# A fifth prefetched expert part, routing by token tile, and an fp32 gather in a two-block network kernel

## The chip, the cores and the metric

The kernel is one launch on one core of a Trainium2 chip. The metric is the device time of that launch in microseconds (us). Before the change three runs took 2184.20, 2184.34 and 2190.19 us, median 2184.34.

## What is computed

The input is 256 tokens of width 1024, all in float32. Two blocks of depth 2 run one after the other. The first block is what this change is about. In each of its two layers:

```python
x = layer_norm(ALPHA * x + mixer(x) @ w_o, ln1_g, ln1_b)        # mixer: attention and gated linear attention, or GQA
aff = softmax(x @ router_w)                                     # 16 experts
gates, idx = top_k(aff.T, 32)                                   # each expert picks its 32 tokens
hid = silu(x[idx] @ w1) * (x[idx] @ w3)                         # per expert 1024 x 1024, twice
ffn = scatter_add((hid @ w2) * gates, idx)                      # 1024 x 1024
ple = sigmoid(x @ ple_gate_w + ple_gate_b) * (p @ ple_w)
x = layer_norm(ALPHA * x + ffn + ple, ln2_g, ln2_b)
```

The second block has, per layer, a feed-forward part, a mixer and another feed-forward part, and ends in one RMS norm: `out = x * rsqrt(mean(x*x) + EPS) * final_norm`.

## The kernel before, in words

Tokens lie on the 128 partitions in two tiles (TILES = 2), so x is [128, 2, 1024]. TensorE (PE) multiplies; a product in exact float32 is one `matmul` in the code and shows in the profile as two records with two weight loads. Where a long product would cost too much that way, both factors are split into a high part, rounded to fp32r, and a low part (value minus high part), and three fp32r products are added: high by high, high by low, low by high. ACT makes high parts (casts), DVE makes low parts (subtractions).

**Weights.** An expert has 12 MiB: six parts of 2 MiB, each 128 partitions by 4096 words. Parts 0 and 1 are the halves of w1, 2 and 3 of w3, 4 and 5 of w2. All weights come through a ring of six slots of 2 MiB (`WeightStream`, L181 issues the loads). SP issues the loads in program order; before a load into a slot it waits on the counter `weights_used`, which PE (or DVE, for a split part) advances when a slot has been read. So a load is issued as soon as the unit six places earlier has been read, and the DMA queue then works off what has been issued.

Expert 1 is special. While routing is still under way nothing can free a slot, so some of its parts go aside, into memory that is free at that time (`aside_places`, with `ASIDE = 4`): part 0 and part 1 into the arena (a general scratch area), part 2 into `mix_cols` and the arena, part 3 into a spare unit that is filled much earlier. Expert 1's parts 4 and 5 use the ring.

**Routing** (L2154 to L2204, L2548 to L2600). After the first layer norm PE multiplies p by ple_w (`ple_products`, 4 results of 512 columns), turns x into columns (L495, eight 128x128 transposes a tile, both tiles together), ACT and DVE split the columns (L504, L520), and 24 products of 16 weight columns and 256 moving columns give the logits (L2555). DVE copies them (L2674), PE turns them, DVE and ACT make the softmax, DVE finds the top 32 by four rounds of MAX8 and MATCH_REPLACE8, and makes the one-hot matrices (`make_hot`), first for experts 0 and 1.

**Gather.** Each expert's tokens are picked by a product of x with the one-hot matrix. Before, x is split for it into `rows_hi` (ACT, L2176, two casts of 2.1 us or more) and `rows_lo` (DVE, L2184, four subtractions). `gather_first` (L2439) picks the tokens of experts 0 and 1 by 32 fp32r products of 256 moving columns, where the 64 wanted columns are repeated four times (`REPEATS`). `gather` (L2453) picks those of all 16 experts by 32 fp32r products of 512 columns, in pieces between the first two experts.

**Experts.** `up` (L2275) is 64 products of 32 weight columns by 256 moving columns, four of which run beside each other on the array; `down` (L2297) 16 of 512; `scatter` (L2307) adds the result into PSUM. After experts 7 and 11 a half of the gate product `x @ ple_gate_w` stands (L2354), its bias added by DVE (L2398, two additions of 128x512 for each half) before ACT's sigmoid.

**The end.** `final_norm`: ACT squares the four halves of x and sums them (L2814), POOL makes both roots together (L2819, L734, L735), DVE scales the two tiles (L3806), SP stores each tile (L3789).

## Time and profile before

| what | value |
|---|---|
| median of 3 runs | 2184.34 us |
| profiled execution, its own time | 2185.28 us |
| its span, first to last instruction | 2183.3 us |
| mean granted PE clock | 0.962 |
| PE busy | 1911.9 us, 88% |
| DVE busy | 1059.3 us, 49% |
| ACT busy | 712.3 us, 33% |
| bytes moved by DMA | 624.05 MB |
| DMA idle or slow around the routing of layer 0 | about 133 to 161 us |
| DMA idle or slow around the routing of layer 1 | about 680 to 742 us |
| experts of layer 0, of layer 1 | about 154 to 602 us, about 738 to 1180 us |

Read it by stretch. In the experts the DMA engines move some 427 GB/s without a break and PE waits for weights; from about 1200 us on (the second block) PE is busy nearly throughout and DMA is half idle. A mean over the span says nothing about either.

### The profile page before, as it was taken

To read this page: it belongs to the slowest core of one execution; us is meant where nothing else is said; L and a number is where in the kernel's file an instruction comes from. 1 tells how busy PE (TensorE), PEld (TensorE's weight loads), DVE (VectorE), ACT (ScalarE), POOL (GpSimd) and SP (SyncE) were. 2 spreads that over 40 slices of the span, in tenths; PEclk is the share of its full clock that TensorE was granted. 3 is DMA by queue.
4 is the path that set the end of the run, shared out by engine and by line. 5 is a ranking of instruction groups with operands and counts; after the bars stand their busy time and mean duration, and the time that the engine had idled before them with its cause. 6 is when DMAs were issued, how large, how long until landed. Compare 5 with 4: busy or idle time off the path is not lost. (4 is left out here: it accounts for less than half of the span.)

```text
span 2183.3 us, 32580 instructions
## 1 busy us (share of the span) xinstructions
PE 1911.9 (88%) x13124; PEld 1354.3 (62%) x13140; DVE 1059.3 (49%) x1607; ACT 712.3 (33%) x1096; POOL 75.6 (3%) x137
## 2 busy tenths in 40 slices
PE   9999667676788986676768999999999999999998
PEld 6765224232366542242324888988888888888887
DVE  4761002010077500020103877787777877787776
ACT  5532002020046210020102433565444433565442
POOL 0000000000010000000000000000000000000000
PEclk9999989998999998898999999999999999999999
DMA  7399999999982899999999655436564655446550
GB/s 243 139 381 427 428 428 423 429 424 427 421 343 72 353 426 430 427 424 428 424 428 398 226 177 205 139 136 212 178 206 155 212 174 201 146 136 207 180 201 19
DMA packets 187952, 624.05 MB, mean 286 GB/s; under 512 B 17655, under 2 KB 129369, under 8 KB 163033
## 3 DMA queue, kind: packets, MB, share of 16 engines
q1 hardware_dynamic: 187864, 622.84, 73.6%
q8 instruction: 61, 1.00, 0.2%
q14 instruction: 27, 0.21, 0.0%
HBM read 621.76 MB, written 1.05 MB: 285 GB/s over the span
## 5 line engine op out<-in xcount | busy, mean ns | idle before, releaser
L3028 PE MATMUL psum<-x_both,up_hi 128*128 128x512 f32 x1408 | 352.9, 393 | 2.5 <-DVE x_both L525 2.2
L2275 PE MATMUL psum<-weight_ring,arena 128*32 128x256 f32 x3840 | 249.5, 411 | 106.7 <-DMA weight_ring<-in_w 106.1
L3028 PEld LDWEIGHTS psum<-x_both,up_hi 128*128 128x128 f32 x1408 | 257.4, 188 | 57.4 <-issue 3.3
L2275 PEld LDWEIGHTS psum<-weight_ring,arena 128*32 128x32 f32 x3840 | 123.5, 116 | 233.8 <-DMA weight_ring<-in_w 133.5
L2415 DVE TENSOR_TENSOR arena<-arena,psum 128x256 f32<-128x256 f32 x32 | 13.5, 421 | 450.6 <-PE psum L2275 450.6
L2297 PE MATMUL psum<-weight_ring,arena 128*32 128x512 f32 x1024 | 148.0, 709 | 73.6 <-DMA weight_ring<-in_w 63.6
L3080 DVE TENSOR_TENSOR up_lo<-weight_ring,up_hi 128x2048 fp32r<-128x2048 f32 x84 | 192.1, 2287 | 13.0 <-ACT up_hi L3051 12.8
L3031 PEld LDWEIGHTS psum<-x_both,up_lo 128*128 128x128 f32 x1408 | 189.4, 188 | 13.5
L3031 PE MATMUL psum<-x_both,up_lo 128*128 128x256 f32 x1408 | 193.2, 280 | 0.0
L3092 DVE TENSOR_REDUCE arena<-psum 128x256 f32<-128x512 f32 x176 | 121.5, 690 | 125.3 <-PE psum L3031 124.2
L652 PE MATMUL psum<-w_lo,x_both 128*128 128x384 f32 (+3 forms) x768 | 170.2, 359 | 2.4 <-DVE mix_lo L793 1.2
L3051 ACT CAST up_hi<-weight_ring 128x2048 fp32r<-128x2048 f32 x84 | 160.1, 1906 | 13.6 <-PE psum L3031 13.4
L3072 ACT ACTIVATE arena<-arena 128x256 f32<-128x256 f32 x88 | 36.7, 418 | 385.9 <-DVE arena L3098 385.9
L2419 DVE COPY arena<-psum 128x512 f32<-128x512 f32 x30 | 20.7, 692 | 283.7 <-PE psum L2297 283.7
L652 PE MATMUL psum<-w_hi,x_both 128*128 128x512 f32 (+3 forms) x640 | 149.2, 365 | 3.5 <-ACT w_hi L613 2.4
L652 PEld LDWEIGHTS psum<-w_lo,x_both 128*128 128x128 f32 x768 | 135.2, 188 | 16.7 <-issue 3.6
L2307 PE MATMUL psum<-arena 128*128 128x512 f32 x240 | 120.2, 648 | 22.2 <-ACT arena L2372 22.2
L3000 PE MATMUL psum<-down_hi,hid_hi 128*128 128x512 f32 x336 | 132.0, 393 | 0.0
L3000 PE MATMUL psum<-down_hi,hid_lo 128*128 128x512 f32 x336 | 131.5, 391 | 0.0
L3000 PE MATMUL psum<-down_lo,hid_hi 128*128 128x512 f32 x336 | 130.5, 389 | 0.0
L2297 PEld LDWEIGHTS psum<-weight_ring,arena 128*32 128x32 f32 x1024 | 31.1, 120 | 155.2 <-DMA weight_ring<-in_w 77.9
L652 PEld LDWEIGHTS psum<-w_hi,x_both 128*128 128x128 f32 x640 | 113.2, 188 | 20.1 <-ACT w_hi L613 3.4
(390 smaller groups left out, 2393.7 us busy)
## 6 DMA issues: line engine op xcount, KB each, us to landing
weight_ring<-in_w SPq DMA_DIRECT2D x184, 2048.0 KB, 25.7
weight_ring<-in_ffn_wg SPq DMA_DIRECT2D x44, 1024.0 KB, 6.0
weight_ring<-in_ffn_wu SPq DMA_DIRECT2D x44, 1024.0 KB, 8.6
weight_ring<-in_ffn_wd SPq DMA_DIRECT2D x44, 1024.0 KB, 5.0
weight_ring<-in_w_in SPq DMA_DIRECT2D x14, 1536.0 KB, 6.7
weight_ring<-in_w_o SPq DMA_DIRECT2D x4, 2048.0 KB, 16.2
arena<-in_w SPq DMA_DIRECT2D x4, 2048.0 KB, 14.9
weight_ring<-in_ple_gate_w SPq DMA_DIRECT2D x4, 2048.0 KB, 25.0
```

The lines of the kernel that those rows point to most:

```text
L652: last = pe.matmul(ps[:, bank, 0:width], x_part[:, cc, a * P:(a + 1) * P], w_part[:, c, :], start=cc == 0 and w_part is high and x_part is ...
L2275: last = pe.matmul(ps[j * CAP:(j + 1) * CAP, 4 + k // 2, 0:QW], tokens[:, cc, :], w[c][:, j * QW:(j + 1) * QW], start=cc == 0, stop=cc == ...
L2297: last = pe.matmul(ps[r * CAP:(r + 1) * CAP, 6 + h, :], hc[:, k, r * CAP:(r + 1) * CAP], w[:, r, h, :], start=k == 0, stop=k == 1)
L2307: last = pe.matmul(ps[:, 2 * a + h, :], back[:, a * P:(a + 1) * P], partial[:, h * BANK:(h + 1) * BANK], start=False, stop=False, skip_gro ...
L2419: dve.tensor_copy(partial[:, BANK:], ps[:, 7, :]).then_inc(part_1.sem, 1)
L3000: last = pe.matmul(ps[:, 2 * h + a, :], x_part[:, f, a * P:(a + 1) * P], w_part[:, f, h * BANK:(h + 1) * BANK], start=False, stop=False, s ...
L3028: last = pe.matmul(ps[:, 4 + 2 * f + h, :], w_part[:, f, h, c, :], x_both[:, :, c, :], start=c == 0, stop=False, skip_group_check=True)
L3031: last = pe.matmul(ps[:, 4 + 2 * f + h, 0:SEQ], w_part[:, f, h, c, :], x_hi[:, c, :], start=False, stop=c == DC - 1, skip_group_check=True)
L3051: act.copy(up_hi[:, k % 2], up_weights(k)).then_inc(hi_up.sem, 1)
L3072: act.activation(silu_g[:, k % 2, :], silu_g[:, k % 2, :], ACT.Silu).then_inc(silued.sem, 1)
L3080: dve.tensor_tensor(up_lo[:, k % 2], up_weights(k), up_hi[:, k % 2].bitcast(F32), ALU.subtract).then_inc(lo_up.sem if k % 2 == 0 else used, 1)
L3092: dve.tensor_reduce(joint[:, f, :], ps[:, 4 + 2 * f + h, :].rearrange("p (t q) -> p q t", t=2), AX, ALU.add).then_inc(joined.sem, 1)
```

## The change

1. **Aside parts.** `ASIDE` is 5: expert 1's part 4 goes aside too, half into `x_cols` as soon as the products of the mixer's output are done, half into `ln_params` after the layer norm. Part 0 is issued earlier, behind p in `mix_out_norm` (its place in the arena is free there because p moved). Expert 0's part 5, the last of the ring before the first expert, is issued last; the slot that it waits for is that of ple_w, whose fourth result PE now makes after the affinities are turned.
2. **Routing by token tiles.** Each token tile is turned, split and multiplied for itself: products of 128 moving columns, 48 of them in place of 24, the products with the high part of x ahead of those with the low part.
3. **Gather in fp32.** `rows_hi` and `rows_lo` are gone; the gather multiplies x itself (fp32, read with a stride of 8 words as weights) by 64 one-hot columns for experts 0 and 1, and by the 448 others later.
4. **Gate bias.** The bias is loaded as one row (4 KB in place of 512 KB spread over the partitions), and PE adds it by two fp32 products of one row for each half, at the head of `gate_products`; DVE's four additions a layer are gone.
5. **The end.** POOL takes a root for each tile as its squares are ready, the gain is scaled by sqrt(D) ahead of time, the four halves are scaled by DVE (three) and ACT (one), and stored one by one.
6. Twenty idle products (which only keep PE busy) become ten; some signals share a name.

```diff
-FIRST, ASIDE = 2, 4
+FIRST, ASIDE, SPARE_PART = 2, 5, 3
...
             load_params(sp, (p_tokens, t["p"][layer, 0].rearrange("(a p) d -> p a d", p=P)))
+            sp.dma_start(Arena(0).take(SLOT), stream.aside[layer][0]).then_inc(signal("aside_unit_0_arrived").sem, 16)
             stream.issue(sp)
...
+        def high_logits(pe, a):
+            for c in range(DC):
+                if c % (DC // 2) == 0:
+                    pe.wait_ge(tile_high.sem, tile_high.at(2 * (2 * a + c // (DC // 2) + 1)))
+                for k, w_part in enumerate((router_hi, router_lo)):
+                    pe.matmul(tile_logits(a), w_part[:, c, :], gate_hi[:, c, a * P:(a + 1) * P],
+                              start=c == 0 and k == 0, stop=False)
...
-                        (bias, spread(t["ple_gate_b"][layer:layer + 1, :])))
+                        (bias[0:1, :], t["ple_gate_b"][layer:layer + 1, :]))
...
+            ple_products(pe, (0, 1))
+            pe.wait_ge(summed_rows.sem, summed_rows.at(0))
+            ple_products(pe, (2,))
+            turn_tile(pe, 0)
+            pe.wait_ge(router_low_kept.sem, router_low_kept.at(1))
+            high_logits(pe, 0)
+            turn_tile(pe, 1)
+            low_logits(pe, 0)
+            high_logits(pe, 1)
+            low_logits(pe, 1)
...
+            for a in range(TILES):
+                pe.matmul(ps[:, 6 + a, :], ident[0:1, 0:1].broadcast_to([1, P]), bias[0:1, h * BANK:(h + 1) * BANK],
+                          start=True, stop=False)
...
-            for a in range(TILES):
-                dve.tensor_tensor(ps[:, 6 + a, :], ps[:, 6 + a, :], bias[:, cols], ALU.add).then_inc(biased.sem, 1)
...
-            for part in (rows_hi, rows_lo):
-                for a in range(TILES):
-                    for c in range(DC):
-                        if part is rows_lo and c % (DC // 2) == 0:
-                            pe.wait_ge(rows_low.sem, rows_low.at(2 * a + c // (DC // 2) + 1))
-                        last = pe.matmul(first_chunks[:, c], part[:, a, c * P:(c + 1) * P],
+            for a in range(TILES):
+                for c in range(DC):
+                    last = pe.matmul(first_chunks[:, c, 0:REPEATS], in_chunks(x[:, a, :])[:, :, c],
...
-                    for part in (rows_hi, rows_lo):
-                        last = pe.matmul(ps[:, c % 4, :], part[:, a, c * P:(c + 1) * P], one_hot[:, a, :],
-                                         start=a == 0 and part is rows_hi,
-                                         stop=a == TILES - 1 and part is rows_lo)
+                    last = pe.matmul(ps[:, c % 4, FIRST * CAP:], in_chunks(x[:, a, :])[:, :, c],
+                                     one_hot[:, a, FIRST * CAP:].bitcast(F32), start=a == 0, stop=a == TILES - 1)
...
-            stream.issue(sp, early[0] + 6)
+            stream.issue(sp, early[0] + 5)
...
+            sp.wait_ge(mixed.sem, mixed.at(0))
+            load_aside(sp, 4, 0)
             tile_ready(sp, 1)
+            load_aside(sp, 1, 0)
+            load_aside(sp, 4, 1)
+            sp.wait_ge(logit_rows.sem, logit_rows.at(1))
+            load_aside(sp, 2, 0), load_aside(sp, 2, 1)
+            issue_early(sp)
...
-            idle_products(pe, 20)
+            ple_products(pe, (3,))
+            idle_products(pe, 10, 0)
...
+            dve.wait_ge(gains.sem, gains.at(1))
+            half_ready(dve, 1, 1)
+            dve.tensor_tensor(gained, half(x, 1, 0), half(ln_params, 0, 0), ALU.mult).then_inc(gains.sem, 1)
+            for a, h in by_vector:
+                dve.wait_ge(rooted.sem, rooted.at(a + 1))
+                dve.scalar_tensor_tensor(out=half(normed, a, h), in0=half(x, a, h), scalar=roots[:, a:a + 1],
+                                         in1=half(ln_params, 0, h), op0=ALU.mult, op1=ALU.mult
+                                         ).then_inc(vector_done.sem, 1)
```

SP's queue of DMA issues at the routing of layer 0, from the slots and the gate bias on, before (arena<-in_w 128x4096 are the aside parts 0 and 1, the two of 128x2048 the halves of part 2, weight_ring<-in_w the ring's expert parts; the branch only ends a block):

```order
L393 DMA arena<-in_c_slots 128x32
L393 DMA arena<-in_ple_gate_b 128x1024
L2519 UNCONDITIONAL_BRANCH
L181 DMA weight_ring<-in_w 128x4096 [waits weights_used]
L2531 DMA arena<-in_w 128x4096 [waits x_tiles_written,weights_used]
L2531 DMA arena<-in_w 128x4096
L2531 DMA mix_cols<-in_w 128x2048 [waits logit_rows_ready]
L2531 DMA arena<-in_w 128x2048
L181 DMA weight_ring<-in_w 128x4096 [waits weights_used] x8
```

and now (x_cols and ln_params take the halves of part 4):

```order
L393 DMA arena<-in_c_slots 128x32
L393 DMA arena<-in_ple_gate_b 1x1024
L2581 UNCONDITIONAL_BRANCH
L2579 DMA x_cols<-in_w 128x2048 [waits half_products_done]
L2579 DMA arena<-in_w 128x4096 [waits x_tiles_written]
L2579 DMA ln_params<-in_w 128x2048
L2579 DMA mix_cols<-in_w 128x2048 [waits logit_rows_ready]
L2579 DMA arena<-in_w 128x2048
L181 DMA weight_ring<-in_w 128x4096 [waits weights_used] x8
```

Part 0 is no longer here: it stands behind p, ahead of two ring units, some rows earlier. Part 4 came in, and the last ring unit of expert 0 went from the head of the aside parts to the head of the last line, whose eight units end with the same one as before.

PE's queue from the ple products to the logits, before (the three rows of L2555 repeat seven more times):

```order
L2162 MATMUL psum<-weight_ring,arena 128x512 x8
L495 MATMUL psum<-ident,x 128x128 x8
L449 MATMUL psum<-zeros_bf 128x512 x2
L495 MATMUL psum<-ident,x 128x128 x8
L2548 UNCONDITIONAL_BRANCH
L2555 MATMUL psum<-gate_hi,router_hi 16x256
L2555 MATMUL psum<-gate_lo,router_hi 16x256
L2555 MATMUL psum<-gate_hi,router_lo 16x256
```

and now (the two of L2211 stand eight times in a row, first for tile 0 and, after the products of tile 0 with the low part, for tile 1; the first piece below is tile 0's head, the second tile 0's last pair, tile 1's turning and what follows):

```order
L2163 MATMUL psum<-weight_ring,arena 128x512 x6
L2189 MATMUL psum<-ident,x 128x128 x8
L2211 MATMUL psum<-gate_hi,router_hi 16x128
L2211 MATMUL psum<-gate_hi,router_lo 16x128
L2211 MATMUL psum<-gate_hi,router_hi 16x128
```

```order
L2211 MATMUL psum<-gate_hi,router_hi 16x128
L2211 MATMUL psum<-gate_hi,router_lo 16x128
L2189 MATMUL psum<-ident,x 128x128 x8
L2218 MATMUL psum<-gate_lo,router_hi 16x128 x8
L2211 MATMUL psum<-gate_hi,router_hi 16x128
```

Two of the eight ple products left this place, and the products with tile 0's high part moved ahead of the turning of tile 1.

PE's queue behind the up products of expert 0, before (the pair of L2453 stands eight times in all):

```order
L2275 MATMUL psum<-weight_ring,arena 32x256 x64
L2477 MATMUL psum<-ident,arena 128x128 x4
L2453 MATMUL psum<-one_hot,rows_hi 128x512
L2453 MATMUL psum<-one_hot,rows_lo 128x512
L2453 MATMUL psum<-one_hot,rows_hi 128x512
```

and now, up to the second expert's down products:

```order
L2329 MATMUL psum<-weight_ring,arena 32x256 x64
L2534 MATMUL psum<-ident,arena 128x128 x4
L2511 MATMUL psum<-one_hot,x 128x448 x8
L2339 MATMUL psum<-ident,arena 64x2x32 x8
L2358 MATMUL psum<-weight_ring,arena 32x512 x16
L2329 MATMUL psum<-arena 32x256 x32
L2329 MATMUL psum<-mix_cols,arena 32x256 x8
L2329 MATMUL psum<-arena 32x256 x8
L2329 MATMUL psum<-spare_unit,arena 32x256 x16
L2511 MATMUL psum<-one_hot,x 128x448 x4
```

The gather stands where it stood, with half as many products.

## Rows read from the trace of the kernel before

**Rows 1.** The page, slices of 54.6 us, and its second group of instructions.
```profile
GB/s 243 139 381 427 428 428 423 429 424 427 421 343 72 353 426 430 427 424 428 424 428 398 226 177 205 139 136 212 178 206 155 212 174 201 146 136 207 180 201 19
...
L2275 PE MATMUL psum<-weight_ring,arena 128*32 128x256 f32 x3840 | 249.5, 411 | 106.7 <-DMA weight_ring<-in_w 106.1
```

**Rows 2.** Windows: stretch, us; busy by engine (x); PEclk, DMA share, GB/s.
```profile
133.50:138.50 5.00, 3.98 (x24) 2.60 (x24) 3.64 (x4) 4.63 (x7) 0.16 (x1) 1.00 0.77 198
138.50:156.50 18.00, 16.26 (x130) 10.27 (x133) 13.99 (x35) 4.48 (x5) 0.00 (x0) 1.00 1.00 425
156.50:161.00 4.50, 4.50 (x88) 2.71 (x84) 0.00 (x0) 0.38 (x1) 0.00 (x0) 1.00 0.93 359
692.70:711.00 18.30, 18.30 (x82) 14.88 (x82) 9.84 (x9) 4.29 (x3) 0.00 (x0) 1.00 0.69 243
711.00:719.50 8.50, 8.45 (x28) 4.34 (x28) 7.71 (x10) 4.36 (x6) 3.42 (x6) 1.00 0.30 91
719.50:739.50 20.00, 17.29 (x135) 11.14 (x139) 15.14 (x36) 6.46 (x9) 0.00 (x0) 1.00 0.96 403
```

**Rows 3.** Timeline of SP's DMA issues, layer 1: start us, duration, engine, line.
```profile
692.74 0.38 SPq L393 DMA_DIRECT2D arena<-in_p  x1
...
719.10 0.95 SPq L2531 DMA_DIRECT2D arena<-in_w  x2
```

**Rows 4.** Ring loads by tile, windows 694:696, 183:186, 766:769, 774:775; issue, then landing.
```profile
L181 SPq DMA_DIRECT2D weight_ring<-in_w x1: 327/327/327, 694.9 to 694.9; - x1
...
DMA to landing us min/median/max: 7.5/7.5/7.5
...
L181 SPq DMA_DIRECT2D weight_ring<-in_w x2: 328/328/328, 183.7 to 185.4; - x2
...
DMA to landing us min/median/max: 11.9/13.5/15.1
...
L181 SPq DMA_DIRECT2D weight_ring<-in_w x2: 327/328/328, 766.9 to 768.6; - x2
...
DMA to landing us min/median/max: 10.9/12.6/14.3
...
L181 SPq DMA_DIRECT2D weight_ring<-in_w x1: 343/343/343, 774.1 to 774.1; - x1
...
DMA to landing us min/median/max: 13.8/13.8/13.8
```

**Rows 5.** Timeline of PE, routing of layer 1: start us, duration us, line, records.
```profile
711.27 7.03 PE L2162 MATMUL psum<-weight_ring,arena 128*128 128x512 f32 x16
...
719.44 1.04 PE L495 MATMUL psum<-ident,x 128*128 128x128 f32 x8
...
721.43 0.28 PE L2555 MATMUL psum<-gate_hi,router_hi 128*16 128x256 f32 x1 [0.96 <-DVE gate_lo L520]
...
732.97 2.15 PE L2439 MATMUL psum<-one_hot,rows_hi 128*128 128x256 f32 x16
```

**Rows 6.** Timeline of DVE, the same place.
```profile
720.60 2.48 DVE L520 TENSOR_TENSOR gate_lo<-psum,gate_hi 128x512 fp32r<-128x512 f32 x4 [1.57 <-ACT gate_hi L504]
...
724.43 0.41 DVE L2674 COPY arena<-psum 16x256 f32<-16x256 f32 x1 [0.26 <-PE psum L2555]
```

**Rows 7.** Timeline of PE, L3431 and L1409; last, L2453's window 161.9:166.
```profile
1437.15 4.13 PE L3431 MATMUL psum<-arena,weight_ring 128*128 128x64 f32 x36
...
57.22 1.95 PE L1409 MATMUL psum<-chunk_masks,ln_params 128*128 128x128 f32 x16
...
161.90:166.00 4.10, 3.98 (x16) 2.93 (x16) 1.00 0.99 408
```

**Rows 8.** Timeline of DVE and of SP at the program's end.
```profile
2172.74 2.73 DVE L3135 SCALAR_TENSOR_TENSOR x<-psum,stat,x 128x512 f32<-128x512 f32 x4 [1.49 <-PE psum L3000]
...
2177.68 2.48 DVE L3806 SCALAR_TENSOR_TENSOR arena<-x,stat,ln_params 128x1024 f32<-128x1024 f32 x2 [2.21 <-POOL stat L735]
...
2178.99 1.54 SPq L3789 DMA_DIRECT2D out<-arena  x2
```

More of the change, by code:

```diff
@@ new lines, in tile_columns, with turn_tile, keep_tile_high @@
+        def tile_columns(columns, a, half):
+            return columns[:, half * DC // 2:(half + 1) * DC // 2, a * P:(a + 1) * P]
+        def turn_tile(pe, a):
+            tile_ready(pe, a)
+            for half in range(2):
+                for c in range(DC // 2):
+                    cc = half * DC // 2 + c
+                    last = pe.transpose(tile_bank(a, half)[:, c, :], x[:, a, cc * P:(cc + 1) * P], ident[:, :])
+                last.then_inc(tile_turned.sem, 1)
+        def keep_tile_high(act, a):
+            for half in range(2):
+                act.wait_ge(tile_turned.sem, tile_turned.at(2 * a + half + 1))
+                act.copy(tile_columns(gate_hi, a, half), tile_bank(a, half)).then_inc(tile_high.sem, 2)
@@ L2292, in down @@
                     more_zeros(pe, zeros)
[L2293 to L2294 removed]
+                if 4 + k < aside:
+                    w = [part[:, r * D:(r + 1) * D].rearrange("p (h n) -> p h n", h=2) for part in aside_places[4 + k]
+                         for r in range(part.shape[-1] // D)]
+                    pe.wait_ge(aside_arrived[4 + k].sem, aside_arrived[4 + k].at(16 * len(aside_places[4 + k])))
+                else:
+                    unit = place_of(slot_unit + 4 + k)
+                    slot = stream.slot(unit)
+                    w = [slot[:, r * D:(r + 1) * D].rearrange("p (h n) -> p h n", h=2) for r in range(4)]
+                    pe.wait_ge(stream.arrived[unit % WEIGHT_SLOTS], arrival(unit))
                 for h in range(2):
@@ L2705, in _ @@
             make_hot(dve, range(FIRST))
-            low_row(dve, 0, 1)
-            for half in range(2):
-                low_row(dve, 1, half)
             make_hot(dve, range(FIRST, EXPERTS))
@@ L3779, in final_norm @@
     def final_norm(block):
-        normed = Arena().take(TILES, D)
+        normed, gained = Arena().take(TILES, D), Arena(TILES * D).take(BANK)
         roots = square_roots
-        rooted, done, stored = (signal(s) for s in ("root_ready", "tokens_scaled", "output_stored"))
+        rooted, gains, stored = (signal(s) for s in ("root_ready", "tokens_gained", "output_stored"))
+        vector_done, scalar_done = signal("vector_halves_scaled"), signal("scalar_half_scaled")
+        half = lambda tile, a, h: tile[:, a, h * BANK:(h + 1) * BANK]
+        by_vector = [(0, 0), (0, 1), (1, 1)]
         @block.sync
```

197 lines of the change are left out of this document (103 added, 94 removed).

## The prediction, made before the changed kernel had run

> **What bounds the kernel.** I read the page's slices first. Moved bytes stand at some 427 GB/s in slices 4 to 11 and 14 to 21 and fall between and after them [rows 1]; the experts' up products waited 106 us for weights in all. So both expert stretches end when the DMA queue has delivered the last weights, and from about 1200 us on PE is the limit. In the DMA-bound part a microsecond of PE, ACT or DVE is worth nothing by itself. What counts is when the DMA queue stands idle, and how many bytes go through it. Then I took windows around both routings, where the ring is full and its slots not yet free. In layer 0 DMA moved 198 GB/s over 5.0 us and 359 over 4.5 us, against 425 between [rows 2]. In layer 1 it is idle far longer: 243 GB/s over 18.3 us, 91 over 8.5 us. Last came the landing times of the ring's loads: a 2 MiB unit takes 2.097 MB / 425 GB/s = 4.9 us of the queue; issued into an idle queue it lands after 7.5 us, and what a landing takes beyond 7.5 is the work still queued ahead of it, the margin by which the release of its slot could come later without a gap [rows 4].
>
> **Part 0 earlier, part 4 aside, one-row bias: layer 0.** The gap of 5.0 us lost (1 - 198/425) x 5.0 = 2.7 us, that of 4.5 us 0.7 us [rows 2]. Part 0, issued some 20 us earlier, fills the first, the extra unit the second. The bias load shrinks from 0.52 MB to 4 KB: 1.2 us of queue. That makes 4.6 us; the small loads (slots, tables for the next layer) still pass through this place at a poor rate, so I take 4.2, with 2.5 and 5.0 as ends. The bytes ahead of the first release grow by one unit (4.9) and the queue is ahead by 3.9, so it runs dry 1.0 us later than before.
>
> **The same in layer 1.** SP issues p at 692.74 and the aside parts at 719.10 [rows 3]. Idle there: (1 - 243/425) x 18.3 = 7.8 us up to 711, and (1 - 91/425) x 8.5 = 6.7 us up to 719.5 [rows 2]. Part 0 (4.9 us) goes into the first, half of part 4 (2.5 us) into the second. But before the first slot is free the queue is dry again, as before: from 719.5 on it has parts 1, 4b, 2 and one ring unit, 7.3 MB or 17.2 us, to about 737.5, while the first slot came free near 739.5. So DMA restarts with the first release, and the gain is one unit that need not come through the ring afterwards, 4.9 us, plus what the first release moves, less gaps that open later.
>
> **When the first slot is free.** Layer 1 before: the second tile is turned from 719.44, the 24 logit products start at 721.43 [rows 5], DVE's four subtractions of 0.62 us start at 720.60, and its copy of the logits at 724.43, 0.26 after their end [rows 6]. Afterwards tile 0's subtractions need not wait for tile 1. DVE is free at 719.4, all four can end at about 722.0, with only four short products left. Logits stand near 722.5 in place of 724.2: 1.7 us. At the gather of the first two experts, 32 products took about 4.1 us (16 in 2.15 us, twice [rows 5]). 16 fp32 products replace them, and the nearest row is L3431, 36 records or 18 products of 64 columns in 4.13 us, 0.23 each [rows 7]: 3.7 us, gaining 0.4 only. The weight loads bound it. By the Trainium skill (TensorE: Matmul & The Clock Gate, LDWEIGHTS) a load takes its columns / 1.2 ns, 107 ns for 128, whatever moves, and an fp32 product has two: this rule speaks against expecting a quarter of the time from a quarter of the columns, and the row (115 ns a record) agrees. The first release comes 2.0 us earlier. The removed splits (ACT, DVE) are hidden otherwise; ple's fourth result moves under DVE's top-32 search and costs nothing.
>
> **A price that no row shows.** The 48 logit products move 128 columns in fp32r; every fp32r product of the trace moves 256 or more. L2555 moves 256 in 0.115 us (721.43 to 724.17, 24 of them). The low end is half of that, 0.06 us. The high end is a product at fp32's rate, L1409: 16 records or 8 products of 128 columns in 1.95 us, 0.24 each [rows 7]. I take the low end, since 16 weight columns leave only the streaming, and hold the other as a rival.
> The Trainium skill (same page, Back-to-back issue gap) gives 81 ns a product in a stream with loads at 128 columns: with it the sum stays, as only four products follow the last subtraction. No run here shows it yet for fp32r.
>
> **The later gather.** 32 fp32r products of 512 columns took 2 x 3.98 = 8.0 us [rows 7]. 16 fp32 ones of 448 take 448/512 of L2162's 7.03/8 = 0.88 us [rows 5], 0.77 each, 12.3 us: 4.4 us more of PE a layer, three quarters (3.3) of it before expert 1's down products are done. Here PE is busy and releases ring slots late. With one more part aside, each ring load also waits for a slot that is read one place later. Layer 1: the seventh load after the first release had 10.9 - 7.5 = 3.4 us of margin; it now waits for the slot read at 768.6 in place of 766.9, plus 3.3: 5.0 later, a gap of 1.6. The eighth had 14.3 - 7.5 = 6.8 and waits for 774.1 in place of 768.6, plus 4.4: 9.9 later, a gap of 3.1 in all [rows 4]. The ninth and later ones have more room. So of the 4.9 us 1.8 are left, and with the 2.0 of the first release layer 1 gains 3.8 (ends 0 and 7). Layer 0: the eighth had 15.1 - 7.5 = 7.6 [rows 4], plus the 1.0 above, less 5.5 + 4.4 - 2.0 = 7.9: 0.7 left, no gap, and the 4.2 stand. It is a narrow fit.
>
> **Gate bias on PE.** Four fp32 products of 512 columns a layer, 4 x 0.88 = 3.5 us of PE, for four additions on DVE: PE waits for DMA in the loops anyway (the 106 us [rows 1]), so nothing either way; without that cover it would be 3.5 us a layer.
>
> **The end.** x is complete at 2172.74 + 2.73 = 2175.5. DVE scales two tiles of 1.24 us from 2177.68, SP issues at 2178.99 and about 2180.2 [rows 8]. Now tile 0's root does not wait for tile 1; DVE has about 0.6 of gain product, then three halves of about 0.65, the last behind tile 1's root near 2177.3, and the last store is issued near 2178.3, half as long. I take 2.0 us, ends 1.2 and 2.6. This is on the path one to one.
>
> **Sum.** 4.2 + 3.8 + 2.0 = 10.0 us off the profiled execution's 2185.3 (span 2183.3 and 2.0 around it): 2175.3. The median of the runs is 0.9 below it, so 2174.4.
>
> **Rivals.**
> A, *short fp32r products at fp32's rate*. For it: the kernel before repeats 64 columns to 256. Against: that gather has 128 weight columns, whose load hides under 256 columns, the router 16. Tile 0's high products take 16 x 0.24 = 3.9 us from about 718.2, then turning 1.0, tile 0's low 1.95, tile 1's high 3.9 and low 1.95: logits at 730.9 in place of 724.2, and with the 0.4 a first release 6.3 later than before. Layer 1: 1.8 - 6.3 = -4.5. Layer 0: 0.7 of room minus 8.3 is a gap of 7.6, 4.2 - 7.6 = -3.4. With the end +2.0: 5.9 us slower, 2190.2. It turns slower once the logits come more than some 3 us late.
> B, *PE too slow behind the first experts*. Reading x as weights with a stride of 8 words is shown by no row; if a load took twice as long, the first gather would take 7.4 us in place of 3.7, and the release would be 1.7 later than before. Layer 0 then 0.7 - 3.7, a gap of 3.0, gains 1.2; layer 1 1.8 - 1.7 = 0.1; the end 2.0: 3.3 us faster, 2181.0. A few waits more in the narrow fits give about the same. The long products hide their loads either way.
> C, *no gap in layer 1*, if the products of 448 columns run nearer their streaming or the margins are larger: 3.1 more, 2171.3.
>
> **Chances.** The forecast 0.56, A 0.21, B 0.17, C 0.06. Its own range is 2171.5 to 2178; to hold 8 in 10 the range reaches from 2170.5 to 2188.5, over C and B and into A. A measurement of this kernel can tell 0.3%, 6.6 us: faster (below 2177.8) 0.60, from the forecast and C less a little; slower (above 2190.9) 0.08, from A's worse half; the rest, B and most of A, 0.32.
>
> **What would show it.** In the changed profile: no stretch below 400 GB/s from 116 to 160 us, part 0 landing before 711 in layer 1, the logits' copy about 1.7 us sooner after x than before, 16 gather records of 64 columns a tile pair at 0.115 us, gather products of 0.77, a short gap of DMA behind the seventh and eighth ring loads of layer 1 and none in layer 0, and the last store about 2 us closer to the last product. I am wrong if L2211 takes 0.2 us or more, if DMA stands still in layer 0 behind the first experts, or if the first experts' end moves without the second block starting earlier.

## The result, and the profile after

The changed kernel is slower: 2190.88 us (median of 20 runs, 2187.59 to 2193.59) against 2185.7 before (20 runs, 2183.08 to 2190.19). The ratio of the two is 1.0024, 95% interval 1.0018 to 1.003: some 5 us lost where 10 were forecast to be gained.

I read the trace after by landmarks, so that the loss has a place: when SP issues p of layer 1 (the end of what layer 0 cost), when PE turns x behind layer 1's experts (L483), and the span. The last three rows are from the experiments below. (p is the small input that is multiplied by ple_w; SP loads it ahead of each layer's routing. A slot is one of the ring's six. The granted clock below is the share of TensorE's full clock, 2.4 GHz, that the profile shows as granted: 1.00 or 0.50 at any moment, between them where a window holds both.)

| kernel | first gather, layer 0: start, length | first slot free, layer 0 | p of layer 1 issued | first slot free, layer 1 | L483 behind layer 1 | span |
|---|---|---|---|---|---|---|
| before | 149.75, 4.1 | 156.51 | 692.74 | 739.72 | 1187.7 | 2183.3 |
| after | 147.85, 7.9 | 159.61 | 695.18 | 745.67 | 1195.5 | 2189.9 |
| e6_contiguous | 148.58, 3.8 | 155.09 | 691.75 | 736.38 | 1183.6 | 2178.1 |
| e8_split_gather | 149.53, 4.1 | 156.15 | 690.48 | 736.09 | 1185.9 | 2180.5 |
| e12 | 148.11, 3.8 | 154.62 | 688.68 | 733.30 | 1179.9 | 2174.6 |

Up to p of layer 1 it is 2.4 us that were lost, in layer 1 another 5.4, and the end gave back 1.2. Of the 2.4 only 1.4 stand at the end of layer 0's experts, where PE turns x (before, then after; e6 has 604.88 there, e8 604.57, e12 602.73). The other 1.0 came in the mixer of layer 1, which the change does not touch:

```profile
606.82 1.06 PE L495 MATMUL psum<-ident,x 128*128 128x128 f32 x8 [0.58 <-DVE x L764]
608.27 1.06 PE L495 MATMUL psum<-ident,x 128*128 128x128 f32 x8 [0.58 <-DVE x L764]
```

(The start of the routing in layer 0 itself varies by 1.2 us from one execution to the next, between kernels that are alike up to there; no single landmark is better than that.)

The place is the gather of the first two experts. PE's timeline after, layer 0 (start us, duration us, engine, line; [idle before <- what ended it]):

```profile
139.77 0.29 PE L2613 MATMUL psum<-ident,arena 16*128 16x16 f32 x2 [0.51 <-DVE arena L2727]
...
147.03 0.82 PE L449 MATMUL psum<-zeros_bf 128*128 128x512 bf16 x3
147.85 7.89 PE L2499 MATMUL psum<-one_hot,x 128*128 128x64 f32 x32
155.53 1.06 PE L449 MATMUL psum<-zeros_bf 128*128 128x512 bf16 x2
156.52 5.83 PE L2329 MATMUL psum<-weight_ring,arena 128*32 128x256 f32 x84
```

It starts 1.9 us sooner than before and takes 7.89 us where the two rows of L2439 took 4.1 [rows 5]. Layer 1 reads the same: 733.30, 7.89 us. That is 0.247 us a record (a product in exact float32 is two records); the forecast had 0.115. The windows after, same columns as [rows 2] (stretch; busy of PE, PEld, DVE, ACT, POOL; granted clock, DMA share, GB/s):

```profile
138.00:142.00 4.00, 3.05 (x28) 1.83 (x26) 2.23 (x9) 0.23 (x1) 0.00 (x0) 1.00 0.56 186
147.90:155.80 7.90, 7.90 (x33) 7.78 (x34) 1.73 (x4) 0.00 (x0) 0.00 (x0) 0.54 1.00 422
155.80:160.00 4.20, 4.20 (x46) 1.77 (x48) 0.00 (x0) 1.87 (x2) 0.00 (x0) 0.65 1.03 441
186.00:206.00 20.00, 19.25 (x215) 11.86 (x213) 1.11 (x2) 6.22 (x14) 0.40 (x1) 1.00 0.87 341
734.00:741.00 7.00, 7.00 (x31) 7.00 (x32) 1.07 (x3) 0.00 (x0) 0.00 (x0) 0.62 0.99 386
741.00:746.00 5.00, 5.00 (x43) 2.06 (x46) 0.00 (x0) 1.87 (x2) 0.00 (x0) 0.51 0.02 3
772.00:792.00 20.00, 19.51 (x216) 12.06 (x214) 1.11 (x2) 5.96 (x13) 0.40 (x1) 1.00 0.84 325
```

Three things are to be seen. First, the loading column: PEld, the loading of weights, is busy throughout the gather (7.78 of 7.90 us). Second, the granted clock is about half there (1.2 GHz in place of 2.4), in both layers, where it was 1.00 before [rows 2]. Third, DMA stands still from 741 to 746 us (3 GB/s), until the first slot is free at 745.67, and is short again some 26 to 46 us behind the first release of each layer (341 and 325 GB/s; the kernel before moves 428 at both places). Layer 0's slow stretch of 5.0 us at 198 GB/s [rows 2] is not gone, it now lies at 138 to 142 us.

What came as forecast: the short fp32r products of L2211 follow each other at 0.06 us (134.77, 134.83, 134.89), and the logits are copied and turned 3.70 us behind the turning of tile 1 in both layers (136.07 to 139.77, 721.52 to 725.22), against 5.5 before.

The end, after: DVE, POOL and SP.

```profile
2180.41 2.73 DVE L3185 SCALAR_TENSOR_TENSOR x<-psum,stat,x 128x512 f32<-128x512 f32 x4 [1.49 <-PE psum L3050]
2183.24 0.69 DVE L3871 TENSOR_TENSOR arena<-x,ln_params 128x512 f32<-128x512 f32 x1
2183.85 1.41 DVE L3874 SCALAR_TENSOR_TENSOR arena<-x,stat,ln_params 128x512 f32<-128x512 f32 x2
2186.03 0.75 DVE L3874 SCALAR_TENSOR_TENSOR arena<-x,stat,ln_params 128x512 f32<-128x512 f32 x1 [0.77 <-POOL stat L3865]
```

```profile
2183.99 1.35 POOL L3863 TENSOR_SCALAR stat<-stat 128x1 f32<-128x1 f32 x1 [0.35 <-ACT arena L2864]
2185.43 0.57 POOL L3865 TENSOR_TENSOR stat<-stat,half_power 128x1 f32<-128x1 f32 x1
```

```profile
2184.62 3.02 SPq L3843 DMA_DIRECT2D out<-arena  x4
```

POOL's addition for the second root shows 1.35 us (the first took 0.32), so the last half waits 0.77 us for it. It ends 0.08 us behind the two halves that DVE scales meanwhile (2185.34 against 2185.26), and so it does in e5 (2177.11 against 2177.03); whether DVE holds it up was not tested. The last store is issued near 2187.3 (the start of the last of four issues that end at 2184.62 + 3.02), 4.2 us behind x (2180.41 + 2.73); before it was 4.7, with a store twice as large [rows 8].

### The profile page after: what moved, and what is told of

Read it like the earlier page. It is cut to its first block and busy times, and to the rows that moved or that the text cites. A ratio compares the mean times of both kernels' runs of the same rounds, so it can differ in the third digit from the quotient of the medians.

```text
span 2189.9 us, 32648 instructions
## 1 busy us (share of the span) xinstructions
PE 1941.5 (89%) x13180; PEld 1373.6 (63%) x13180; DVE 1047.4 (48%) x1593; ACT 703.9 (32%) x1093; POOL 82.0 (4%) x139
## 5 line engine op out<-in xcount | busy, mean ns | idle before, releaser
L2358 PE MATMUL psum<-weight_ring,arena 128*32 128x512 f32 x992 | 142.0, 704 | 65.8 <-DMA weight_ring<-in_w 56.7
```

The source lines that it names most:

```text
L2358: last = pe.matmul(ps[r * CAP:(r + 1) * CAP, 6 + h, :], hc[:, k, r * CAP:(r + 1) * CAP], w[r][:, h, :], start=k == 0, stop=k == 1)
```

## The experiments

The first five ask why the gather is slow, the others what the rest of the change is worth and what is left when the gather is not slow. Before ran beside each of them, at medians of 2185.1 to 2186.4.

**e1_idle20.** Ten idle products had been taken out ahead of the gather. Are they what kept the clock up?

```diff
-            idle_products(pe, 10, 0)
+            idle_products(pe, 20, 0)
```

> The changed kernel with 20 idle products behind ple's fourth result in place of 10. In the changed kernel the granted clock is 0.50 from about 148.6 to 158.9 us and again about 735 to 745 us, and the first gather takes 7.9 us instead of 3.7. Theory 1 (the gather itself, 16 fp32 products of 64 columns bound by weight loads, is too little work for PE to keep its clock): the clock falls all the same, the gather takes 7.9 us, and the time is that of the changed kernel or up to 2 us more, 2190 to 2193. Theory 2 (the missing ten idle products ahead of it let the clock fall): clock 1.00 through both gathers, 3.7 us each, first releases about 3 us earlier (1 to 2 us are lost since PE reaches the turned ranks late), and 2182 to 2187 in all.

2193.86 us (6 runs), ratio to before 1.0039 [1.0026, 1.0051]. The gather takes 7.88 us as without them, and the clock falls all the same (0.51 from 151 to 160 us). The ten products too few are not what makes the gather slow. They may have a part in when the clock falls: 2.1 and 3.9 us behind the gather's start in the two layers, against 0.6 and 2.3 in the changed kernel, in one trace of each. But they also put the gather of layer 1 1.3 us later (39.4 us behind p against 38.1).

**e2_between.** An idle product behind every second product of the gather, to keep PE busy in it.

```diff
+                    if c % 2 and (a, c) != (TILES - 1, DC - 1):
+                        idle_products(pe, 1, 0)
```

> The changed kernel with one idle product of 512 bf16 columns behind every second product of the first gather (7 in all). Theory 1 (the gather's own thin work): clock 1.00 through the gather, which takes 16 x 0.23 + 7 x 0.22 = 5.2 us in place of 7.9, up of expert 0 at 7.1 us in place of 8.2 and 9.0, first releases 3.5 to 4.5 us earlier, and 2182 to 2187. Theory 2 (idle products missing ahead): the clock falls as before, the gather takes some 10 us, and the time is 1 to 4 us above the changed kernel's.

2190.03 us (11 runs), 1.002 [1.0011, 1.0029]. Layer 1 of this run is the most telling place of the study. PE's timeline, and two windows of it:

```profile
739.96 0.95 PE L2499 MATMUL psum<-one_hot,x 128*128 128x64 f32 x4
740.75 0.38 PE L449 MATMUL psum<-zeros_bf 128*128 128x512 bf16 x1
740.96 0.95 PE L2499 MATMUL psum<-one_hot,x 128*128 128x64 f32 x4
```

```profile
738.00:742.00 4.00, 4.00 (x19) 3.39 (x20) 2.38 (x7) 0.00 (x0) 0.00 (x0) 1.00 1.05 442
742.00:747.00 5.00, 5.00 (x27) 4.88 (x26) 0.00 (x0) 0.00 (x0) 0.00 (x0) 1.00 0.85 315
```

The clock stays at 1.00 through the whole gather, and it is no faster: four records and one idle product repeat each 1.00 us (739.96, 740.96). So the low clock does not make the gather slow. (The whole takes 8.2 us with the seven idle products in it, and the records between two of them start 0.24 us apart as in after.) In layer 0 of the same run the clock still fell.

**e3_first_fp32.** The kernel before with nothing but the new first gather: 16 fp32 products that read x.

```diff
-            for part in (rows_hi, rows_lo):
-                for a in range(TILES):
...
+            for a in range(TILES):
+                for c in range(DC):
+                    last = pe.matmul(first_chunks[:, c, 0:1], in_chunks(x[:, a, :])[:, :, c],
```

> The kernel before, with only the first gather changed: 16 fp32 products of 64 columns from x (the split rows are still made for the later gather, which is as before). Twenty idle products stay ahead of it. Theory 1: the clock falls to 0.50 within about 2 us of the gather's start in both layers, the gather takes near 7.9 us in place of 4.1, the first slot is released about 4 us later, and the time is 2 to 7 us above the kernel before. Theory 2: clock 1.00, the gather takes 3.7 us, time within 2 us of the kernel before.

2196.81 us (5 runs), 1.0053 [1.0039, 1.0066], the slowest of all. The gather takes 7.90 and 7.89 us here too, in the old surroundings, with the same rate at a clock of 0.99 as at 0.50. The loads before and behind 152.9 us start 0.24 us apart and take 335 ns (duration: min/median/max, then first and last start):

```profile
150.00:153.00 3.00, 3.00 (x13) 2.80 (x12) 3.00 (x5) 0.00 (x0) 0.00 (x0) 0.99 0.96 410
153.00:158.00 5.00, 5.00 (x23) 5.00 (x23) 1.96 (x5) 0.00 (x0) 0.00 (x0) 0.50 0.93 388
```

```profile
L2436 PEld LDWEIGHTS psum<-one_hot,x x12: 312/335/336, 150.2 to 152.8; 128*128 128x128 f32 x12
L2436 PEld LDWEIGHTS psum<-one_hot,x x21: 334/335/340, 152.8 to 157.6; 128*128 128x128 f32 x21
```

DMA moves 61 GB/s from 157 to 163 and 107 from 745 to 751 us. One change alone therefore carries the whole loss and more. None of the theories in the expectations of e1 to e3 named what was left after them, the weight load itself; with this stride the low clock is not what makes it slow.

**e6_contiguous.** After, but the weights are 128 neighbouring columns of x.

```diff
-                    last = pe.matmul(first_chunks[:, c, 0:REPEATS], in_chunks(x[:, a, :])[:, :, c],
+                    last = pe.matmul(first_chunks[:, c, 0:REPEATS], x[:, a, c * P:(c + 1) * P],
```

> The kernel after, whose first gather reads 128 neighbouring columns of x as weights in place of every eighth column (same number of products, same moving columns; the output is another one, since other columns are picked for the first two experts). Theory 'stride': a weight load that reads every eighth word takes about 0.24 us a record, a contiguous one 0.115, so the 32 records take 3.7 us in place of 7.9, the granted clock stays at 1.00 to the end of the first up products, first releases come near 155 and 741 us in place of 159.6 and 745.7, and the time is 8 to 9 us below after's 2190.9, near 2182. Rival 'moving data': fp32 products of 64 moving columns cost this at any stride (one-hot columns out of a broadcast view, or fp32 itself); then the gather stays at 7.9 us and the time at 2190.9.

2182.7 us (11 runs), 0.9985 [0.9976, 0.9994], 8.2 us below after. The loads and products of the gather, after and here (duration ns: min, median, max):

```profile
L2499 PEld LDWEIGHTS psum<-one_hot,x x64: 313/335/340, 147.8 to 740.7; 128*128 128x128 f32 x64
L2499 PE MATMUL psum<-one_hot,x x64: 401/443/451, 147.8 to 740.7; 128*128 128x64 f32 x64
```

```profile
L2499 PEld LDWEIGHTS psum<-one_hot,x x64: 186/192/192, 148.6 to 733.3; 128*128 128x128 f32 x64
L2499 PE MATMUL psum<-one_hot,x x64: 275/275/323, 148.6 to 733.4; 128*128 128x64 f32 x64
```

The load is 335 ns against 192, which is what L3431 shows as well, and the gather takes 3.79 us (32 records, 0.118 each, the forecast's 0.115). The clock stays at 1.00 in the window that was at 0.54:

```profile
147.90:155.80 7.90, 7.60 (x89) 5.50 (x91) 2.38 (x7) 1.87 (x2) 0.00 (x0) 1.00 0.99 415
```

From the start of the gather to the first free slot it is 6.51 us in both layers, against 11.76 and 12.37 after. Of the differences of 5.25 and 5.86, 4.10 are the loads. The other 1.15 and 1.76 are idle and first up products at the lower clock (in layer 1 those start at 741.97 and free the slot at 745.67, 3.70 us; here 1.99): that is what the clock costs, two layers together 2.9 us. Of this kernel and of after there is one trace each; e10 and e12, which load the same way, kept 1.00 in the gather too.

**e7_strides.** The same place with a stride of 2 words in layer 0 and of 4 in layer 1.

```diff
+            s = 2 + 2 * layer
+            return x[:, a, c // s * s * P:(c // s + 1) * s * P].rearrange("p (q s) -> p q s", s=s)[:, :, c % s]
...
-                    last = pe.matmul(first_chunks[:, c, 0:REPEATS], in_chunks(x[:, a, :])[:, :, c],
+                    last = pe.matmul(first_chunks[:, c, 0:REPEATS], near_columns(a, c),
```

> The kernel after, whose first gather reads its weight columns with a stride of 2 words in layer 0 and of 4 words in layer 1 (other columns are picked for the first two experts, so the output is another one). Theory 'stride', all or nothing: any stride above 1 gives 0.24 us a record, 7.9 us in both layers. Rival, in proportion: a record of stride 2 takes about 0.12 to 0.15 us (4 to 5 us in layer 0), one of stride 4 about 0.24 or something between (5 to 8 us in layer 1). If the stride does nothing, both layers show 7.9 with no relation to it, and e6_contiguous too.

One run, 2184.43 us. Its two gathers:

```profile
148.18 6.18 PE L2503 MATMUL psum<-one_hot,x 128*128 128x64 f32 x32
...
728.89 7.73 PE L2503 MATMUL psum<-one_hot,x 128*128 128x64 f32 x32
```

So 32 records take 3.79 us contiguous, 6.18 at 2 words, 7.73 at 4, 7.89 at 8. But the 6.18 us hold two rates. The clock fell 1.1 us into this gather, at 149.3 us, and in layer 1 0.7 us into it. The loads before and behind that moment, layer 0 and then layer 1, and windows on either side (columns as above, the clock third from the right; a load under way at the cut stands in both lines):

```profile
L2503 PEld LDWEIGHTS psum<-one_hot,x x10: 193/196/242, 148.2 to 149.2; 128*128 128x128 f32 x10
L2503 PEld LDWEIGHTS psum<-one_hot,x x24: 196/331/336, 149.1 to 153.8; 128*128 128x128 f32 x24
...
L2503 PEld LDWEIGHTS psum<-one_hot,x x4: 307/329/329, 728.9 to 729.6; 128*128 128x128 f32 x4
L2503 PEld LDWEIGHTS psum<-one_hot,x x30: 329/329/330, 729.3 to 736.1; 128*128 128x128 f32 x30
```

```profile
148.20:149.20 1.00, 1.00 (x9) 1.00 (x9) 1.00 (x2) 0.00 (x0) 0.00 (x0) 1.00 0.96 410
149.50:151.50 2.00, 2.00 (x11) 2.00 (x11) 0.49 (x2) 0.00 (x0) 0.00 (x0) 0.50 0.98 414
...
728.90:729.50 0.60, 0.60 (x3) 0.60 (x3) 0.60 (x2) 0.00 (x0) 0.00 (x0) 1.00 1.03 437
730.00:735.00 5.00, 5.00 (x23) 5.00 (x23) 0.71 (x2) 0.00 (x0) 0.00 (x0) 0.50 1.04 439
```

At the full clock a load at 2 words takes 196 ns, the contiguous one of e6 192; records start 0.118 us apart against 0.112. At the low clock the load at 2 words takes 331 ns and records start 0.213 apart. At 4 words it is 329 ns and 0.233 at either level. So with the full clock 2 words cost next to nothing and 4 words nearly the whole price of 8: the step lies between 8 and 16 bytes. The Trainium skill has a rule for this (SBUF — State Buffer, Door 1: The DMA port swizzle, in its note on SBUF "cachelines"): lines of 16 bytes, and at least two hits on a line for full bandwidth. The trace agrees with both, since 4 and 8 words, one hit each, cost nearly the same, and 2 words, two hits, almost nothing at the full clock. It disagrees with four fp32 words being a stride "for free" (7.73 us against 3.79).

Why the clock fell in layer 0 of this run stays open: the loads still took 196 ns when it did, and e6 kept 1.00 at nearly the same pace. Slow loads cannot be the whole cause of the fall.

**e4_later_fp32.** Before, with only the later gather in fp32.

```diff
-                    for part in (rows_hi, rows_lo):
-                        last = pe.matmul(ps[:, c % 4, :], part[:, a, c * P:(c + 1) * P], one_hot[:, a, :],
...
+                    last = pe.matmul(ps[:, c % 4, FIRST * CAP:], in_chunks(x[:, a, :])[:, :, c],
+                                     one_hot[:, a, FIRST * CAP:].bitcast(F32), start=a == 0, stop=a == TILES - 1)
```

> The kernel before with one change: the later gather multiplies x in fp32 (strided weights) by the 448 one-hot columns of the other experts, 16 products a layer for 32 in fp32r. Theory of the prediction: 0.77 us a product, 4.4 us more of PE a layer, and without a fifth part aside most of it fits the margin of the ring's landings (3.4 and 6.8 us); a gap of about 1 us a layer, 2186 to 2188. Rival 'free': PE waits for weights anyway, 2185.7. Rival 'full price': the ring follows PE one to one there, 4.4 us a layer, 2194.

2188.21 us (11 runs), 1.0011 [1.0002, 1.002]: 3.0 us above before, where the prediction's theory gave about 1 us a layer; nearer to it than to either rival (nothing, or 4.4 us a layer). Eight products take 6.30 us, 0.79 each (forecast 0.77), although they too load with the stride of 8 words: a load of 0.24 us hides behind 448 moving columns.

**e5_final.** Before, with only the new end (the diff is point 5 of the change).

> The kernel before with the change's final_norm alone. In the changed kernel the stretch from the last state of x to the end of the span is about 1.1 us shorter than before, not the 2.0 forecast. Both theories on the clock say nothing of it: I expect 1.0 to 1.4 us less than the kernel before (ratio 0.9995), and POOL's second root at about 1.35 us for its first step where it runs beside DVE. If the 2.0 of the forecast were right for this part alone, it would be 2 us less.

2183.02 us (11 runs), 0.9992 [0.9983, 1.0001]. From L483 to the end of the span it is 994.4 us against 995.6, a gain of 1.2 us, as in after (994.4); the medians give 2.35 (against 2185.37 beside it) with an interval that takes in no gain.

**e8_split_gather.** After, with both gathers as before from rows_hi and rows_lo, and so with four parts aside. All else of the change stays.

```diff
-FIRST, ASIDE, SPARE_PART = 2, 5, 3
+FIRST, ASIDE, SPARE_PART = 2, 4, 3
...
+            high_row(act, 0)
...
-            for a in range(TILES):
-                for c in range(DC):
+            for part in (rows_hi, rows_lo):
+                for a in range(TILES):
```

> The kernel after with the gather of before: x is split into high and low rows again (they take the place of part 4, so four parts are aside as before) and both gathers are products of fp32r; routing by token tiles, the early part 0, the one-row bias and the new end stay. Theory: the whole loss was the first gather; with it gone the first slot is free about 1.7 us earlier than before in each layer, DMA follows it in layer 1 and saves the bias's 1.2 us in layer 0, the end gives 1.1 to 1.6: 5 to 7 us below before's 2185.7, 2179 to 2181. Rival: the early part 0 and the small loads behind it cost layer 0 its time (a gap of DMA at 138 to 142 us), and the fifth part was worth more than the routing: 2184 to 2187.

2184.39 us (11 runs), 0.9994 [0.9985, 1.0003]: 6.5 us below after, and not to be told from before. The rival was right. DMA runs short around the first release of layer 0 (289 GB/s) and ahead of that of layer 1 (192 GB/s; the first slot is free at 736.09):

```profile
138.00:142.00 4.00, 2.70 (x28) 1.60 (x25) 2.92 (x7) 2.53 (x4) 0.00 (x0) 1.00 0.52 181
...
155.80:160.00 4.20, 4.20 (x84) 2.49 (x80) 0.00 (x0) 0.38 (x1) 0.00 (x0) 1.00 0.83 289
...
734.00:741.00 7.00, 6.91 (x128) 4.06 (x128) 0.39 (x2) 1.70 (x3) 0.00 (x0) 1.00 0.56 192
```

An earlier part 0 without a fifth part only makes the queue dry sooner; the fifth part is what the early issue needs to be worth anything, and the fifth part needs the place of rows_hi and rows_lo.

**e9_early_constants.** e8 with the four small loads of the next layer's constants issued near 113 us in place of 128. What makes the slow stretch at 138 to 142 us? The DMA view of after over 127 to 142 us, in 40 slices of 0.38 us:

```profile
GB/s 481 437 437 393 393 481 393 481 393 481 437 306 481 481 437 437 393 393 481 393 481 350 524 393 350 481 481 393 481 350 393 27 38 21 60 72 296 288 247 236
DMA packets 1136, 5.46 MB, mean 364 GB/s; under 512 B 786, under 2 KB 786, under 8 KB 787
```

More than two thirds of the packets are under 512 bytes, and from about 138.6 us five slices in a row, 1.9 us, move 21 to 72 GB/s. Those packets are the constants' loads, issued at 128 us, and the slots.

```diff
+            if layer == 0:
+                load_odd_constants(sp)
             sp.wait_ge(job.x_made.sem, job.x_made.at(2))
...
             sp.wait_ge(mixed.sem, mixed.at(0))
-            if layer == 0:
-                load_odd_constants(sp)
```

> e8_split_gather with the four small loads of the next layer's constants (gqa norms, positions, frequencies) issued near 113 us, ahead of p, where DMA moves only 150 to 270 GB/s, in place of 128 us. In e8 they pass near 139 us, where DMA moves 181 GB/s over 4 us: some 2.3 us of queue. Theory 'the first slot decides': with four parts aside the queue is dry before the first slot is free (292 GB/s in 155 to 160 us), so the time saved is lost again there: 2184, as e8. Rival 'one to one': every place saved counts, 2182.

2188.14 us (11 runs), 1.0008 [0.9999, 1.0016]. Against the kernel before beside each of them it is 1.7 us above and e8 0.8 below (the two intervals overlap a little): neither of the two theories. The hole moved with the loads, into the weights that the mixer's output waits for:

```profile
122.00:130.00 8.00, 4.77 (x24) 3.65 (x23) 1.23 (x2) 0.55 (x1) 0.00 (x0) 1.00 0.75 289
```

(e8 moves 426 GB/s there.) That is (1 - 289/425) x 8.0 = 2.6 us of the queue, and the gather starts 3.0 us later than in e8 (152.55 against 149.53).

**e10_contiguous_early_constants.** The same edit on e6.

> e6_contiguous (five parts aside, the first gather reads neighbouring columns, so other columns are picked for the first two experts) with the same four small loads issued near 113 us. In e6 the stretch from 138 to 142 us moves 217 GB/s, the queue is full from there through the first release at 155.1. Theory 'the small loads are what is left of layer 0's gap': 2 us less, 2180.7, and 138 to 142 us above 350 GB/s; layer 1's p is issued near 690 in place of 691.75. Rival 'the gap is made by something else' (the wait of part 1 for the second tile): 2182.7 as e6, and the stretch stays slow.

2183.42 us (12 runs), 0.9994 [0.9984, 1.0004], no better than e6. The stretch 138 to 142 us is full now (428 GB/s), but the routing is 3.3 us later (gather at 151.90), for the same reason as in e9, and the queue still had 2.6 us of earlier work to do there. So this run does not show by itself that the small loads had made the hole; e11 and e12 are the better test.

**e11_constants_in_hole and e12_contiguous_constants_in_hole.** The four loads directly behind ple_w near 103 us, in e8 and in e6. The queue is dry soon after.

```diff
+            stream.issue(sp, out_job.first + 3)
+            load_odd_constants(sp)
             stream.issue(sp, out_job.first + 2 + EVEN_BLANKS)
...
             sp.wait_ge(mixed.sem, mixed.at(0))
-            if layer == 0:
-                load_odd_constants(sp)
```

> e8_split_gather with the four small loads issued directly behind ple_w near 103 us. In e9 they were issued at 113 us, behind weights that the queue then had, and their price only moved there (287 to 289 GB/s in 122 to 130 us) and held up what the mixer's output waits for. Here the queue is dry soon after (209 GB/s in 110 to 114 us), so they should pass unpaid. Theory 'unpaid, but the first slot decides': routing starts as in e8, the queue is dry longer before the first slot at 156 us, the time stays near 2184. Rival 'unpaid and one to one': 2182. Third case, they hold up the routing as in e9: 2188.

> e6_contiguous (its first gather picks other columns for the first two experts) with the same move of the four small loads. Here the queue is full through the first release, so 2 us saved at 138 to 142 us should be kept: 2180.7 in place of 2182.7, p of layer 1 issued near 690. If it stays at 2182.7, something behind the first release takes it back (the landings' margin in the ring, as in 188 to 204 us, where e10 moved 345 GB/s).

e11: 2184.89 us (11 runs), 0.9995 [0.9986, 1.0004], as e8: the time saved is lost again before the first slot (213 GB/s from 155 to 160 us). e12: 2180.2 us (11 runs), 0.9978 [0.9969, 0.9987], 2.5 us below e6, where 2.0 were expected. Its windows, at the places of the first fence of windows, and one more, at 760 us:

```profile
138.00:142.00 4.00, 3.04 (x32) 1.93 (x30) 2.40 (x8) 0.39 (x2) 0.00 (x0) 1.00 0.76 263
147.90:155.80 7.90, 7.60 (x95) 5.70 (x98) 1.98 (x6) 1.87 (x2) 0.00 (x0) 1.00 1.01 423
155.80:160.00 4.20, 4.20 (x79) 2.42 (x68) 0.13 (x1) 0.39 (x1) 0.00 (x0) 1.00 1.03 439
186.00:206.00 20.00, 19.19 (x189) 11.87 (x182) 1.11 (x2) 5.46 (x11) 1.14 (x3) 1.00 0.99 408
...
760.00:780.00 20.00, 18.94 (x214) 11.55 (x212) 1.11 (x2) 6.53 (x14) 0.40 (x1) 1.00 0.85 333
772.00:792.00 20.00, 18.71 (x180) 9.93 (x176) 0.42 (x1) 2.81 (x6) 0.75 (x2) 1.00 0.95 397
```

Two things are to be read from them. The stretch at 138 to 142 us is still not full: 263 GB/s lose 1.5 us, where e6 (217) lost 2.0; e11 (296) loses 1.2, where e8 lost 2.3. So the four small loads made only a part of the hole, and what makes the rest was not traced. And the first slot of layer 1 is free at 733.30, so that 760 to 780 us lies as far behind it as 772 to 792 does in after: the gap of 325 GB/s in after is there with the fast gather too.

e12 is no kernel to keep, since its first two experts get other columns. Of those that compute the reference, none is faster than before by more than the measurement can tell; e5, e8 and e11 beat after. What would be wanted is five parts aside and a gather that reads neighbouring columns (or, by the first loads of e7, pairs within 16 bytes, as long as the clock stays), that is a copy of x in the order of the chunks (8 KB a partition) beside part 4 (16 KB). I found no free place for it and did not try one.

## Why the prediction was wrong, point by point

By landmarks, forecast against measured, in us off the profiled execution of before:

| | forecast | after | e6 | e12 |
|---|---|---|---|---|
| layer 0 (p of layer 1) | -4.2 | +2.4 | -1.0 | -4.1 |
| layer 1 (L483, less the row above) | -3.8 | +5.4 | -3.1 | -3.7 |
| the end | -2.0 | -1.2 | -1.1 | -0.9 |
| span | -10.0 | +6.6 | -5.2 | -8.7 |

The profiled executions of e6 and e12 were the fastest of their 11 runs, so their columns say too much: by medians e6 gains 2.5 us and e12 4.9 (interval 2.8 to 6.8), and these are the surer numbers. In which row the excess lies is not known.

1. **The step that failed: "16 fp32 products replace them ... 0.23 each: 3.7 us. The weight loads bound it."** The weight loads do bound it, but with a stride of 8 words each takes 0.247 us, not 0.115, and the gather 7.9 us. The nearest row, L3431, loads neighbouring words. I had written the right mechanism and number down as rival B (7.4 us for the gather) and given it 0.17.
2. **Rival B was itself too cheap.** It had the release 1.7 us later than before and 3.3 us still gained. Measured, the first slot came 3.1 us later in layer 0 and, from p on, 3.5 in layer 1. The gather took 0.5 more than 7.4, and the granted clock fell, 1.2 and 1.8 us, which stood in no term. In layer 0 the late release opened the gap that the forecast had put at none: 341 GB/s over 186 to 206 us are 4.0 us, against 0.8 in e12 (408). And e6 against after shows the exchange rate: 5.25 and 5.86 us of later release, 11.1 together, are 8.2 us of median and 11.8 of span. By the table 3.4 of the 11.8 lie in layer 0 and 8.5 in layer 1. In layer 1 DMA stands still until the first slot is free, as the prediction says, so each microsecond counts in full there; what the 2.6 us beyond that are was not traced.
3. **"Part 0, issued some 20 us earlier, fills the first" gap: wrong.** The hole merely moved from 133.5 to 138 us. In part it is made by small loads that pass slowly, and they need their time wherever there is work behind them (2.6 us in e9). The prediction named them and took 0.4 us for them; let pass where the queue is dry, they give back 0.5 to 1.1 us of the hole (e12 against e6, e11 against e8). The rest of the hole is not explained. e12 reaches the 4.2 us of the forecast in layer 0 (4.1 at L495 already), more than its fuller windows account for, in one execution that was the fastest of its kernel.
4. **Layer 1: right in the sum, once the gather is, and not in its terms.** e6 gains 3.1 and e12 3.7 of the 3.8. But the gap behind the seventh and eighth loads is larger than forecast: 333 GB/s over 760 to 780 us in e12 are (1 - 333/425) x 20 = 4.3 us, forecast 3.1. The first release came 2.4 us sooner in e12, forecast 2.0 (from p on, 44.6 us against 47.0). The forecast's 4.9 less 4.3 plus 2.4 is 3.0, so 0.7 of the 3.7 stand in no term, and part of the agreement is luck. (The prediction's queue in layer 1 would have run out at 719.5 + 17.2 = 736.7, not 737.5; nothing hangs on it.)
5. **The end: 1.2 for 2.0,** at the low end of its range. The second root's first step on POOL took 1.35 us, and the last half waited for it.
6. **Right:** the logits 1.7 us sooner (1.8), 0.06 us for a short fp32r product, so rival A is false; 0.77 us for a later product (0.79). That the gate bias costs nothing was not tested: no run takes it by itself.

The range ended at 2188.5, short of the time: A bounded it, and B had been priced as a smaller gain.

## What to carry to other kernels

When a product's weights are read with a stride, look for a row that loads with that stride before taking a price, and if there is none, give the slow case its full chain (late release, dry queue, lower clock) and not only its own microseconds. A short moving side exposes the load: with 64 columns the stride cost 4.1 us, with 448 next to nothing (0.79 us a product, 0.77 forecast). When two runs are compared, look at the granted clock in each before a difference is put down to the edit: the 6.18 us of e7 are half clock, not stride. Before filling a gap in DMA, look at what is in it: many small packets are work, and moving them only helps if they go where the queue is dry. And when a gap is looked for in another run, move the window with the event that it follows.

## What the runs showed of the hardware

- A weight load of 128 fp32 columns, in a stream of products with 64 moving columns, at granted clock 1.00: 192 ns with neighbouring words (e6), 196 with a stride of 2 words (e7), 329 with 4 (e7), 335 with 8 (e3); the records start 0.112, 0.118, 0.234 and 0.238 us apart. At 0.50 the loads at 4 and 8 words take the same, and that at 2 words takes 331 ns.
- The granted clock fell to 0.50 in or shortly into the first gather in after, e1 and e3 (both layers), e2 (layer 0) and e7 (both), and stayed at 1.00 in e6, e10, e12 and in layer 1 of e2, while PE shows 100% busy; the busy share of PE in the profile does not foretell it. With more idle products ahead it fell later (e1), and in e7 it fell while the loads were still fast. What decides it is open.
- In e9, 736 packets under 512 bytes lie in the 8 us from 122 to 130, where the queue moves 289 GB/s in place of 426. The Trainium skill (DMA: Bandwidth & Descriptors, Specifications) asks for 512 bytes for line rate; the trace agrees.
